# A new opening for a two-layer decoder trunk: input in two transfers, first projection regrouped, identity products on TensorE

## The reference, cut to what matters

```python
def rmsnorm(x, g):
    y = x * lax.rsqrt(jnp.mean(x * x, axis=-1, keepdims=True) + RMS_EPS)
    return y * g

h = rmsnorm(x, g[0])                       # layer 0
u = h @ w_in                               # 1024 x 3088
pool_u, z, xbc, dt_raw = u[..., :o1], u[..., o1:o2], u[..., o2:o3], u[..., o3:]
xbc = silu(causal_dwconv(xbc, conv_w) + conv_b)
dt = softplus(dt_raw + dt_bias)            # 16 heads
```

## Time and profile before

| | |
|---|---|
| median of 3 runs | 959.81 us (959.0 to 961.54) |
| profiled execution, its own time | 962.23 us |
| span in the profile | 960.5 us |
| busy: TensorE, VectorE, ScalarE, GpSimd | 902.9, 667.1, 472.7, 268.6 us |
| DMA | 153.74 MB, 160 GB/s over the span |
| mean granted TensorE clock | 0.98 |

### The profile page before, as it was taken

One profiled execution on the slowest core, in us unless ns is written; L12 is line 12 of the kernel. 1 busy time (PEld: TensorE's weight loads), 2 busy tenths in 40 slices (PEclk: granted clock), 3 DMA queues, 4 the chain that ended last, 5 costly groups with the idle time before them and its releaser, 6 DMA issues.

```text
span 960.5 us, 17149 instructions
## 1 busy us (share of the span) xinstructions
PE 902.9 (94%) x7268; PEld 878.1 (91%) x7268; DVE 667.1 (69%) x1030; ACT 472.7 (49%) x661; POOL 268.6 (28%) x195
## 2 busy tenths in 40 slices
PE   6999998899989999999999988999998699999997
PEld 6899988798979999999799988899898699999996
DVE  6897988777287555555779999967676385555553
ACT  5545544565355444444553333646464364454543
POOL 1000817243142000000468687346341340000000
PEclk9999999999999999999999999999999899999999
DMA  8454434544455555655555554245442445655551
GB/s 286 133 176 133 149 114 134 174 133 132 132 175 182 192 189 186 195 186 183 162 165 181 180 173 125 96 137 169 156 133 88 132 132 182 202 191 193 190 184 45
DMA packets 81031, 153.74 MB, mean 160 GB/s; under 512 B 6251, under 2 KB 7227, under 8 KB 80955
## 3 DMA queue, kind: packets, MB, share of 16 engines
q1 hardware_dynamic: 80843, 152.60, 49.9%
q10 hardware_dynamic: 112, 0.05, 0.0%
HBM read 151.58 MB, written 1.05 MB: 159 GB/s over the span
## 4 chain that ended last, share of the span: by engine, by line
PE 64%; DVE 24%; ACT 4%; issue 3%; POOL 3%; DMA 2%; DVEq 0%; POOLq 0%; ACTq 0%
PE ps L501 20%; PE ps L503 20%; PE ps L502 19%; DVE ps L1643 5%; DVE w_lo L1279 4%; ACT w_hi L927 2%; POOL w_lo L1916 2%; DVE E L1450 1%; DVE xc L1351 1%; DMA raw<-in_mlp_w 1%; DVE xT L1591 1%; PE ps L743 1%; PE ps L745 1%; PE ps L744 1%; PE ps L568 1%
## 5 line engine op out<-in xcount | busy, mean ns | idle before, releaser
L927 ACT ACTIVATE w_hi<-raw 128x1024 fp32r<-128x1024 f32 x284 | 296.9, 1055 | 255.8 <-DMA raw<-in_mlp_w 138.4
L501 PE MATMUL ps<-h_hi,w_hi 128*128 128x256 f32 x1280 | 363.8, 284 | 27.9 <-issue 13.7
L1279 DVE TENSOR_TENSOR w_lo<-raw,w_hi 128x1024 fp32r<-128x1024 f32 x210 | 274.1, 1324 | 129.5 <-ACT w_hi L927 129.3
L502 PE MATMUL ps<-h_lo,w_hi 128*128 128x256 f32 x1280 | 360.9, 282 | 0.0
L503 PE MATMUL ps<-h_hi,w_lo 128*128 128x256 f32 x1280 | 360.9, 282 | 0.0
L501 PEld LDWEIGHTS ps<-h_hi,w_hi 128*128 128x128 f32 x1280 | 247.1, 193 | 31.9 <-issue 17.8
L502 PEld LDWEIGHTS ps<-h_lo,w_hi 128*128 128x128 f32 x1280 | 247.3, 193 | 0.0
L503 PEld LDWEIGHTS ps<-h_hi,w_lo 128*128 128x128 f32 x1280 | 247.1, 193 | 0.0
L1916 POOL TENSOR_TENSOR w_lo<-raw,w_hi 128x1024 fp32r<-128x1024 f32 x74 | 183.0, 2494 | 99.4 <-ACT w_hi L927 99.4
L1939 POOL TENSOR_TENSOR rfac<-stat,mhalf 128x2 f32<-128x2 f32 (+1 forms) x14 | 16.6, 1182 | 457.1 <-DVE stat L1573 326.1
L501 PE MATMUL ps<-r_hi,w_hi 128*128 128x256 f32 x512 | 144.3, 282 | 0.0
(11 more groups left out here) (247 smaller groups left out, 1291.7 us busy)
## 6 DMA issues: line engine op xcount, KB each, us to landing
raw<-in_mlp_w SPq DMA_DIRECT2D x128, 512.0 KB, 3.8
raw<-in_cd_w_in SPq DMA_DIRECT2D x40, 512.0 KB, 3.7
raw<-in_xa_wkv SPq DMA_DIRECT2D x32, 512.0 KB, 4.0
raw<-in_ab_w_in SPq DMA_DIRECT2D x24, 512.0 KB, 3.9
raw<-in_xa_wq SPq DMA_DIRECT2D x16, 512.0 KB, 3.8
raw<-in_xa_wo SPq DMA_DIRECT2D x16, 512.0 KB, 3.8
raw<-in_cd_w_out SPq DMA_DIRECT2D x16, 512.0 KB, 3.7
raw<-in_ab_w_out SPq DMA_DIRECT2D x12, 512.0 KB, 3.8
```

The costliest lines, as they stand in the source:

```text
L501: nc.tensor.matmul(dst, wt[0], x[0], start=start, stop=False, skip_group_check=True)
L502: nc.tensor.matmul(dst, wt[0], x[1], start=False, stop=False, skip_group_check=True)
L927: nc.scalar.activation(w_hi[:, v % SLOTS, :, :], raw[:, v % SLOTS, :, :], ACT.Copy)\
L1279: V.tensor_tensor(w_lo[:, v % SLOTS, :, :], raw[:, v % SLOTS, :, :], f(w_hi[:, v % SLOTS, :, :]), ALU.subtract).then_inc(lo_ready_dve, 1)
```

## The change

The input comes in two transfers of 512 channels each, the second behind unit 0 in SyncE's queue. TensorE makes seven identity products before the gains' transposes and three after the first half's transposes, all into the first bank of `("xbc", 0)`, which is cleared by the first real product. Unit 0's products come before the second half's transposes. The first segment's products are grouped: per block four hi*hi (they wait for w_hi and h_hi), four w_lo*hi (for w_lo), four w_hi*lo (for h_lo). ScalarE and VectorE read the transposed input from the banks; VectorE's copies to `xT` come after all of `h_lo` and after the `w_lo` of unit 4, and ScalarE's squares still come after the rounding of unit 4. The `dt` products stand behind unit 4's products instead of in front of them.

```diff
--- before.py
+++ after.py
@@ -38,6 +38,7 @@
 
 P = 128
 SLOTS = 6
+WARM = (7, 3)
 POOL_WINDOWS = (2, 4, 8, 16)
 RMS_EPS, LN_EPS = 1e-6, 1e-5
 
@@ -361,9 +362,9 @@
         ps = ctx.enter_context(nc.psum_tensor("ps", [P, 8, 512], F32))
 
 
-        x_landed, gain_landed, mem_landed, vec_landed, ssm_landed, poolw_landed, out_stored = (
-            sem(n) for n in ("x_landed", "gain_landed", "mem_landed", "vec_landed", "ssm_landed", "poolw_landed",
-                             "out_stored"))
+        x_landed = [sem("x_left_landed"), sem("x_right_landed")]
+        gain_landed, mem_landed, vec_landed, ssm_landed, poolw_landed, out_stored = (
+            sem(n) for n in ("gain_landed", "mem_landed", "vec_landed", "ssm_landed", "poolw_landed", "out_stored"))
         raw_landed = [sem(f"raw_landed{i}") for i in range(SLOTS)]
         hi_ready, lo_ready_dve, lo_ready_pool = (sem(n) for n in ("hi_ready", "lo_ready_dve", "lo_ready_pool"))
 
@@ -446,7 +447,12 @@
 
         @block.sync
         def _(sp_):
-            sp_.dma_start(xtok[:, :, :], A["x"][0].rearrange("(t p) d -> p t d", p=P)).then_inc(x_landed, 16)
+            def x_half(g):
+                c = slice(512 * g, 512 * g + 512)
+                sp_.dma_start(xtok[:, :, c], A["x"][0][:, c].rearrange("(t p) d -> p t d", p=P))\
+                    .then_inc(x_landed[g], 16)
+
+            x_half(0)
 
             def later_inputs():
                 for name, v in MISC_ROWS:
@@ -472,6 +478,8 @@
                 if u >= SLOTS:
                     sp_.wait_ge(pe_made, after("pe", "unit", u - SLOTS))
                 sp_.dma_start(raw[:, u % SLOTS, :, :], units[u]).then_inc(raw_landed[u % SLOTS], 16)
+                if u == 0:
+                    x_half(1)
             for i in range(4):
                 hf, t = i // 2, i % 2
                 sp_.wait_ge(dve_made, after("dve", "otok", i))
@@ -587,13 +595,55 @@
                 return [s_[:, t * P:(t + 1) * P] for t in range(TT)]
 
 
+            def first_projection(us):
+                seg = ("xbc", 0)
+                for ui in us:
+                    u = first[seg] + ui
+                    for i in range(2):
+                        kt = 2 * ui + i
+                        for part in range(3):
+                            if part == 0:
+                                pe.wait_ge(hi_ready, u + 1)
+                                pe.wait_ge(act_made, after("act", "h", "in0", kt))
+                            elif part == 1:
+                                pe.wait_ge(*lo_wait(u))
+                            else:
+                                pe.wait_ge(dve_made, after("dve", "h", "in0", kt))
+                            for n in range(4):
+                                dest = seg + (n // 2,)
+                                st = kt == 0 and part == 0 and n % 2 == 0
+                                if st and n:
+                                    acquire(dest)
+                                wt, x = unit_w(u, i, n)[part == 1], h_src(kt)[part == 2]
+                                ends = kt == J - 1 and part == 2
+                                mm = nc.tensor.matmul(bank2(dest)[:, n % 2, :], wt, x, start=st, stop=ends,
+                                                      skip_group_check=True)
+                                if ends and n == 1:
+                                    mm.then_inc(*finish(dest))
+                    if ui == 3:
+                        mm.then_inc(*finish(seg + (1,)))
+                        L.also("pe", "unit", u)
+                    else:
+                        mm.then_inc(pe_made, tick("pe", "unit", u))
+
+            def warm(n):
+
+                for _ in range(n):
+                    nc.tensor.matmul(bank(("xbc", 0, 0))[:, 0:P], ident[:, :], ident[:, :], start=True, stop=True,
+                                     skip_group_check=True)
+
             pe.wait_ge(pool_made, after("pool", "ident"))
+            acquire(("xbc", 0, 0))
+            warm(WARM[0])
             pe.wait_ge(gain_landed, 16)
             transposes(("gains",), [(0, stage[0:96, 0, :], 96)])
-            pe.wait_ge(x_landed, 16)
             for i in range(4):
+                pe.wait_ge(x_landed[i // 2], 16)
                 transposes(("xT", i), [((c * TT + t) * P, xtok[:, t, (2 * i + c) * P:(2 * i + c + 1) * P], P)
                                        for c in range(2) for t in range(TT)])
+                if i == 1:
+                    warm(WARM[1])
+                    first_projection([0])
 
             def h_ready(tag):
                 def ready(kt):
@@ -601,19 +651,21 @@
                 return ready
 
 
-            project(("xbc", 0), [("xbc", 0, 0), ("xbc", 0, 1)], h_src, ready=h_ready("in0"), tail=0)
+            first_projection([1, 2, 3])
             pe.wait_ge(pool_made, after("pool", "r0"))
             rows(("R0",), [rfac[:, 0, t:t + 1] for t in range(TT)])
             pe.wait_ge(vec_landed, 16 * (2 + len(MISC_ROWS)))
             transposes(("vecs",), [(P, stage[0:MISC_N, 1, :], MISC_N), (2 * P, stage[:, 2, :], P),
                                    (3 * P, stage[0:DWN - P, 3, :], DWN - P)])
+            xbc1 = [("xbc", 1, 0), ("xbc", 1, 1)]
+            project(("xbc", 1), xbc1, h_src, only=[0])
             pe.wait_ge(dve_made, after("dve", "wdtg"))
             acquire(("dt",))
             for j in range(J):
                 mm = nc.tensor.matmul(ps[0:HEADS, use[("dt",)][0], 0:T], wdtg[:, j, :], xT[:, j, :],
                                       start=(j == 0), stop=(j == J - 1))
             mm.then_inc(*finish(("dt",)))
-            project(("xbc", 1), [("xbc", 1, 0), ("xbc", 1, 1)], h_src)
+            project(("xbc", 1), xbc1, h_src, only=[1, 2, 3])
             pe.wait_ge(act_made, after("act", "dtT"))
             acquire(("dtT",))
             for t in range(TT):
@@ -946,10 +998,15 @@
                     .then_inc(act_made, tick("act", "h", tag, j))
 
             for j in range(J):
-                round_to(j // 2 + 1)
-                h_part("in0", 0, 0, j)
-
-            act.wait_ge(x_landed, 16)
+                if j % 2 == 0:
+                    round_to(j // 2)
+                    act.wait_ge(*full(("xT", j // 2)))
+                nc.scalar.activation(h_hi[:, j, :], bank2(("xT", j // 2))[:, j % 2, :], ACT.Identity,
+                                     scale=gain(0, 0, j)).then_inc(act_made, tick("act", "h", "in0", j))
+
+            round_to(4)
+            for g in range(2):
+                act.wait_ge(x_landed[g], 16)
             for t in range(TT):
                 if t:
                     own()
@@ -1294,18 +1351,17 @@
             V.memset(mhalf[:, :], -0.5).then_inc(dve_made, tick("dve", "mhalf"))
             V.memset(upad[:, :, :, 0:3], 0.0).then_inc(dve_made, tick("dve"))
             V.memset(pu[:, :, 0:16], 0.0).then_inc(dve_made, tick("dve", "pads"))
+            for j in range(J):
+                if j % 2 == 0:
+                    low_to(j // 2)
+                dve.wait_ge(act_made, after("act", "h", "in0", j | 1))
+                V.scalar_tensor_tensor(out=h_lo[:, j, :], in0=bank2(("xT", j // 2))[:, j % 2, :], scalar=gain(0, 0, j),
+                                       in1=f(h_hi[:, j, :]), op0=ALU.mult, op1=ALU.subtract)\
+                    .then_inc(dve_made, tick("dve", "h", "in0", j))
+            low_to(4)
             for i in range(4):
-                dve.wait_ge(*full(("xT", i)))
                 V.tensor_copy(xT[:, 2 * i:2 * i + 2, :], bank2(("xT", i))).then_inc(dve_made, tick("dve", "xTc", i))
                 freed("dve", ("xT", i))
-                for c in range(2):
-                    L.also("dve", "x", "in0", 2 * i + c)
-            dve.wait_ge(act_made, after("act", "gains"))
-            low_to(0)
-            for j in range(J):
-                low_h("in0", 0, 0, j)
-                if j % 2 == 1:
-                    low_to(j // 2 + 1)
             for t in range(TT):
                 dve.wait_ge(act_made, after("act", "ss0", t))
             V.tensor_scalar(stat[:, 1, 0:2], stat[:, 0, 0:2], 1.0 / D, RMS_EPS, ALU.mult, ALU.add)\
```

## The result

The changed kernel took 964.8 us in the median of 8 runs (962.19 to 967.9), the kernel before 960.73 us in 8 (959.0 to 964.16) on the same chip. The ratio is 1.0044, 95% interval 1.0029 to 1.0058: slower by 4.1 us. The forecast was 961.0 us, at most 963.8. The profiled execution of the changed kernel took 965.68 us.

What follows compares the result with a forecast made beforehand. The prediction held that the end follows how early the dt products end, through VectorE's chain from 32.06 us. It summed -0.4 and +1.8 to +1.4, took +1.2: 959.8 + 1.2 = 961.0 us, range 957.8 to 963.8.

Steps and rivals of the forecast that it cites:

- input halves and unit 4's landing: Opening: left half at about 4.8 us, right half at 7.4; unit 4 rounded at 17.1 us.
- R0 gated by unit 4, squares and copies: Opening: R0, the row of the input's factor, starts at 23.0 us against 25.88, after a TensorE stall.
- the 2.9 us won at R0: Opening: R0's gain goes into unit 4's 24 products, now ahead of dt; dt ends at 30.3 us against 30.66.
- the hinge: VectorE's w_lo of unit 7, at 32.06 us before; foretold at 31.4 to 32.0 us.
- the new wait at bank 5 of 2.8 us: Near 43 us: TensorE waits about 2.8 us for VectorE to free bank 5 for the memory's last four transposes.
- Rival (c): TensorE was the bound all along, so reaching dtT 3.0 us earlier lasts to the end: 956.8 us; chance 0.09.
- Rival (d): Opening: identity products do not raise the clock, which rises at 18 us as before: 962.9 us; chance 0.07.
- The -0.4 us: Opening: dt products end 0.4 us earlier, and VectorE's chain from 32.06 us moves by as much.
- The fall at bank 5: TensorE's clock falls around the wait near 43 us: 1.9 plus 0.3 us, less 0.4 absorbed by ScalarE: +1.8 us.
- rival (b): The clock falls at R0 too, on the slow side, adding another 1.9 us: 962.9 us; chance 0.20.
- VectorE's chain from 32.06 us moves by as much: VectorE has no wait ended by TensorE from 32.06 to 140 us, so it follows the dt products: -0.4 us.
- the rule that the prediction cited: Trainium skill: transposes do not count as TensorE work for raising the clock; makes the fall near 38.6 to 43.1 us nearly certain.

Runs made afterwards that it cites:

- b_late046: Kernel before with two identity products (0.46 us) in front of the dt products: 962.58 us, 1.0015 of before.
- b_fill: Kernel before with identity products in five later TensorE waits for normed input (about 186, 275, 473, 690, 764 us): 956.0 us, 0.9960 of before.
- b_fill_again: Kernel before with the five later stalls filled with identity products, run once more unchanged: 959.2 us, 0.9968 of before.
- a_again: The changed kernel once more, nothing altered: 965.74 us, 1.0041 of before.
- a_late046: Changed kernel with two identity products (0.46 us) in front of the dt products: 966.74 us, 1.0061 of before.
- a_nowarm: Changed kernel without its ten identity products in the opening: 962.68 us, 1.0007 of before.
- a_factor_early: Changed kernel with the input's factor made before ScalarE rounds unit 4 and VectorE makes its w_lo: 963.45 us, 1.0030 of before.
- a_warm70: Changed kernel with the seven identity products but without the three behind the second input transposes: 963.64 us, 1.0030 of before.
- b_warm7: Kernel before with seven identity products ahead of the gains' transposes: 962.28 us, 1.0004 of before.
- b_late115: Kernel before with five identity products (1.15 us) in front of the dt products: 963.11 us, 1.0017 of before.
- a_nowarm_late: Changed kernel without the opening's identity products, but with two (0.46 us) in front of the dt products: 964.09 us, 1.0035 of before.
- a_dtfirst: Changed kernel with the dt products in front of unit 4's products again: 966.48 us, 1.0050 of before.
- a_fill: Changed kernel with identity products in five later TensorE waits for normed input (about 186, 275, 473, 690, 764 us): 959.34 us, 0.9982 of before.
- a_fill_open: a_fill with identity products also before R0 (7) and before the memory's last transposes (12): 959.12 us, 0.9982 of before.

## Why the prediction was wrong

**Right.** The opening in the profiled execution, step by step: input halves and unit 4's landing; identity products without cost in front of the first product; R0 gated by unit 4, squares and copies (22.75 us); the 2.9 us won at R0 spent on unit 4's products ahead of dt; -0.5 us at the hinge for -0.4; the new wait at bank 5 of 2.8 us. Rival (c), TensorE as the bound all along, fell: TensorE reached dtT 3.1 us earlier (38.58 against 41.70) and nothing of it was left. Rival (d) fell too: the first four products ran at the upper clock.

**The -0.4 us** came out (-0.5) and was still not what the change is worth. It is a difference to one execution of before, the one in which the products were slow up to 18 us. In three of the five other profiles of the old opening without identity products ahead of it, b_late046, b_fill and b_fill_again, transposes had already raised the clock, and there the hinge is 1.3 to 1.4 us earlier (b_late046 less its 0.46 us). Over four profiles each the changed opening is 0.7 us behind at the hinge and 1.2 us behind at 140 us. That this is what the prediction added up for the opening, +1.2 us, is luck: one term was too low and the other too high.

**The fall at bank 5**, +1.8 us, is an event that comes only in some executions, and the term is mostly too large. Of the ten profiles that have this stall unfilled, four have no fall behind it (the changed kernel, a_again, a_late046, a_nowarm) and six have one; of the six only a_factor_early paid 1.8 us, the others 0.8 to 1.1. Likewise rival (b)'s fall at R0: there in a_again's and a_warm70's profiles, not in the first. Being alternatives of one execution and not of the kernel, they should have gone into the sum as shares, not one into the forecast and one into a rival.

**The step that failed** is the one that made the sum the whole answer: "VectorE's chain from 32.06 us moves by as much", and with it the end. The prediction had the rows that warn of this. It used, two stalls of 3.15 and 3.18 us with the low clock behind one of them only, to price the new stall at bank 5, and did not ask what a shift of the opening does to these two and to the third at 472 us. The term that is missing is about +3 us, the measured +4.1 less the forecast +1.2: more of the low level behind waits that the change did not touch. In the table of the stalls it is 7.0 us more, which is 3.5 us at half speed; between the filled kernels the changed one is 0.2% behind in place of 0.44%, so that the fills take 2 of the 4 us away. In the profiled pair it is the fall at 141 us (+0.6 us from there to 190) and above all the stall at 275 us (+3.1 us between 278.5 and the start after the next stall). Over eleven kernels without filled stalls the mean span follows the time at the low level with a correlation of 0.94, 0.39 us for each us of it. Among them are the changed kernel and five variants of it that came out slower than before, and one, a_nowarm, that did not; at the hinge they all lie within 2.1 us of each other.

| kernel | ratio | at the low level, us |
|---|---|---|
| before | 1 | 36.3 |
| b_warm7, b_late115, b_late046 | 1.0004, 1.0017, 1.0015 | 37.4, 38.3, 38.6 |
| a_nowarm | 1.0007 | 38.4 |
| a_factor_early | 1.0030 | 42.2 |
| a_nowarm_late | 1.0035 | 43.7 |
| a_warm70 | 1.0030 | 44.7 |
| changed, a_late046, a_dtfirst | 1.0044, 1.0061, 1.0050 | 45.3, 46.7, 49.2 |
| a_fill, b_fill | 0.9982, 0.9960 | 23.8, 23.6 |

**What stays open.** Shown is that filling the later stalls takes their falls away and brings the changed kernel below the kernel before; that it takes about half of the distance between the two kernels away, 0.44% to 0.2%; and that among the kernels without fills the time follows the low level. The other half is there with the fills, and the profiles put it ahead of 140 us. Not shown is by what rule a given opening leads to more or fewer falls, nor why the fall at 141 us comes with the changed opening; no row of before gave the sign. Nor is it settled how large the rest between the filled kernels is (1.8 us, give or take 1.4), and what sets the pace of 0.115 or 0.118 us.

## What to carry to other kernels

Ahead of a forecast for an early edit, list the later stalls of TensorE of 2 us and more and see which have the low clock behind them; if like stalls differ, an edit that shifts them by some tenths of a microsecond can cost or give some us without touching them, and the range has to say so. Filling such stalls with products that compute nothing, some less than the stall is long (3.06 us in one of 3.15), took 0.3% to 0.4% off the kernel before, and with them in place the identity products of the opening made no difference any more; filling the shorter and the uncertain ones too gave nothing more. Compare openings only once the later stalls are filled, with the mean granted clock of all executions beside the times. One profile of before is one draw as well: where a term of the sum is a difference to it, such as a stretch of slow products, read a second profile before pricing it.

## What was not expected of the hardware

- Identical code lets the granted clock fall in one execution and not in another: behind R0's wait it did in a_again (1.84 us) and not in the changed kernel's first profile (1.67 us), behind bank 5's it did in a_warm70 (2.81 us) and not in the changed kernel (2.80 us), and at 483 us it did in b_fill and not in b_fill_again. A wait of 2.1 us (475 us) was enough in five of the eight changed kernels without fills. Even among the executions of one kernel the times spread over 955.87 to 965.21 us (kernel before).
- Transposes alone raised the clock (b_late046, b_fill, b_fill_again), against the rule that the prediction cited. The sixteen took 3.33 to 3.55 us there, and 3.67 us in before, whose first products were slow.
- An identity product is two instructions, and each costs 0.21 to 0.24 us at the lower clock (six in 1.26 us, fourteen in 3.35) and 0.12 us at the upper one (26 in 3.06 us in a_fill). Where the clock is low in spite of them they overrun: the last group in a_fill, at 759.91 us, took 5.32 us in place of 3.06:

```profile
186.97 3.06 PE L839 MATMUL ps<-ident 128*128 128x128 f32 x26
...
759.91 5.32 PE L839 MATMUL ps<-ident 128*128 128x128 f32 x26
```

- The pace of back-to-back products at a granted clock of 1.00 has more than one value, 171 or 174 in 20 us, for the same code (a_fill_open and a_fill).
